# Weight blocks of block one's up-projections written 160 words apart, at another place for each pair, and low activations at another distance in each stage

## The reference

```
def swiglu(x, w_gate, w_up, w_down):
    return (jax.nn.silu(x @ w_gate) * (x @ w_up)) @ w_down

for l in range(DEPTH):                       # block one; DEPTH = 2, D_MODEL = 1024, D_FF = 2816
    h = layer_norm(ALPHA * h + 0.5 * swiglu(h, ffn1_w_gate[l], ffn1_w_up[l], ffn1_w_down[l]), ...)
    proj = h @ w_in[l]                       # state space, two attention mixers
    ...
    h = layer_norm(ALPHA * h + mix, ...)
    h = layer_norm(ALPHA * h + 0.5 * swiglu(h, ffn2_w_gate[l], ffn2_w_up[l], ffn2_w_down[l]), ...)
```

## The kernel before

| operand | start | from block k to k+1 |
|---|---|---|
| `w_hi`, `w_lo` | 128, 0 | 512 bytes, so 0 |
| `x_hi`, `x_lo` (272 or 274 columns) | 192, 64 | 288 words = 1152 bytes, so 128 |
| `plain_hi`, `plain_lo` | 192, 64 | 1152 bytes, so 128 |
| `xt_hi`, `xt_lo` (256 columns) | 64, 64 | 1024 bytes, so 0 |
| `hid_hi`, `hid_lo` (272 columns, down-projections) | 128, 0 | 1088 bytes, so 64 |

## Time and profile before

### The profile page before, as it was taken

One profiled execution on the slowest core, in us unless ns is written; L12 is line 12 of the kernel. 1 busy time (PEld: TensorE's weight loads), 2 busy tenths in 40 slices (PEclk: granted clock), 3 DMA queues, 4 the chain that ended last, 5 costly groups with the idle time before them and its releaser, 6 DMA issues.

```text
span 1951.3 us, 42291 instructions
## 1 busy us (share of the span) xinstructions
PE 1938.8 (99%) x16150; PEld 1899.9 (97%) x16150; DVE 1429.2 (73%) x2591; ACT 1020.5 (52%) x1527; POOL 152.7 (8%) x192
## 2 busy tenths in 40 slices
PE   9999999999999999999999999999999999999998
PEld 9999989999999999899999999999999999999998
DVE  6774787987688758879878875667765775667763
ACT  4443687554455446865546444565445444565443
POOL 0001123000100011320010100000000000100000
PEclk9999999999999999999999999999999999999999
DMA  7454433545454544345553665435564555435554
GB/s 264 172 199 167 165 109 121 182 172 191 154 187 172 186 162 162 109 151 194 187 201 130 230 235 196 152 134 191 193 221 177 194 202 208 151 130 194 194 213 153
DMA packets 46830, 346.66 MB, mean 178 GB/s; under 512 B 5344, under 2 KB 6416, under 8 KB 9232
## 3 DMA queue, kind: packets, MB, share of 16 engines
q1 hardware_dynamic: 44416, 335.63, 47.7%
q0 software_dynamic: 2320, 9.74, 1.5%
HBM read 344.29 MB, written 1.07 MB: 177 GB/s over the span
## 4 chain that ended last, share of the span: by engine, by line
PE 91%; DVE 4%; ACT 2%; DVEq 1%; issue 1%; ACTq 0%; DMA 0%; SPq 0%; POOL 0%
PE ps L595 29%; PE ps L596 29%; PE ps L597 29%; DVE w_lo L1938 1%; PE ps L1111 0%; DVE pj L2399 0%; DVE cst L2420 0%; PE ps L1146 0%; DVE pj L2396 0%; ACT scratch L1615 0%; DVE scratch L2365 0%; PE ps L936 0%; DMA raw<-in_w_up 0%; PE ps L947 0%; ACT w_hi L1246 0%
## 5 line engine op out<-in xcount | busy, mean ns | idle before, releaser
L1938 DVE TENSOR_TENSOR w_lo<-raw,w_hi 128x1024 fp32r<-128x1024 f32 (+1 forms) x582 | 749.6, 1314 | 153.7 <-ACT w_hi L1246 149.7
L1246 ACT ACTIVATE w_hi<-raw 128x1024 fp32r<-128x1024 f32 (+1 forms) x582 | 635.3, 1122 | 118.9 <-PE ps L597 99.3
L595 PE MATMUL ps<-x_hi,w_lo 128*128 128x256 f32 (+3 forms) x2416 | 684.5, 283 | 1.5 <-DVE x_lo L2030 0.6
L596 PE MATMUL ps<-x_lo,w_hi 128*128 128x256 f32 (+3 forms) x2416 | 675.7, 280 | 0.0
L597 PE MATMUL ps<-x_hi,w_hi 128*128 128x256 f32 (+3 forms) x2416 | 675.2, 279 | 0.0
L595 PEld LDWEIGHTS ps<-x_hi,w_lo 128*128 128x128 f32 x2416 | 454.5, 188 | 9.2 <-issue 5.5
L596 PEld LDWEIGHTS ps<-x_lo,w_hi 128*128 128x128 f32 x2416 | 454.0, 188 | 0.8
L597 PEld LDWEIGHTS ps<-x_hi,w_hi 128*128 128x128 f32 x2416 | 454.6, 188 | 0.0
L595 PE MATMUL ps<-hid_hi,w_lo 128*128 128x256 f32 (+1 forms) x1536 | 431.4, 281 | 0.0
L597 PE MATMUL ps<-hid_hi,w_hi 128*128 128x256 f32 (+1 forms) x1536 | 430.2, 280 | 0.0
L596 PE MATMUL ps<-hid_lo,w_hi 128*128 128x256 f32 (+1 forms) x1536 | 429.8, 280 | 0.0
(11 more groups left out here) (330 smaller groups left out, 1554.7 us busy)
## 6 DMA issues: line engine op xcount, KB each, us to landing
raw<-in_w_up SPq DMA_DIRECT2D x176, 1024.0 KB, 4.8
raw<-in_w_down SPq DMA_DIRECT2D x64, 1408.0 KB, 6.0
raw<-in_w_in SPq DMA_DIRECT2D x36, 1024.0 KB, 4.8
raw<-in_w_out SPq DMA_DIRECT2D x16, 1024.0 KB, 4.8
cst<-row_copy POOLq DMA_DIRECT2D x2, 1088.0 KB, 8.5
raw<-in_w_up SPq DMA_DIRECT2D x4, 512.0 KB, 6.7
cst<-in_consts POOLq DMA_DIRECT2D x1, 1537.5 KB, 7.1
prm<-in_prm POOLq DMA_DIRECT2D x2, 690.0 KB, 7.6
```

What stands on the lines that cost most here:

```text
L595: mm(dst, w_lo[:, j, cols], xa, start=first, stop=False)
L596: mm(dst, w_hi[:, j, cols], xb, start=False, stop=False)
L1246: fn(w_hi[:, j, c], raw[:, j, c], ACT.Copy).then_inc(hi_done, 1)
L1938: v.tensor_tensor(w_lo[:, j, c], raw[:, j, c], w_hi[:, j, c].bitcast(F32), ALU.subtract)\
```

## The change

Three things, all in block one's four up-projections.

1. Where the weights' blocks lie. Before, the blocks of a unit stand 128 words apart at the unit's start. Now `placed(turn, j)` gives for the pairs of turns 1 to 10 of each stage (pair n = 0 to 19) a pitch and two offsets, one for `w_hi` and one for `w_lo`. For n below 16 the pitch is 160 words, and the offsets are n modulo 4 and n divided by 4, in units of 64 bytes: each of the 16 combinations once. For n = 16 to 19 the pitch is 128 words, the high offset 0, the low offset 0 to 192 bytes. Turn 0's two pairs and everything outside these stages stay at pitch 128 and offset 0. The second unit of a pair now lies 1408 words (`W_WIDE`) behind the first everywhere. ScalarE and VectorE write the same 1024 words a unit, in these stages as 8 blocks of 128.
2. Where the low activations lie. `plain_lo` starts 2304 words plus 5, 7, 7 or 6 times 64 bytes behind `plain_hi`, by level 0 to 3 (layer 0's ffn2, layer 1's ffn1, layer 1's ffn2, the crossing to block two), where it was 6 times in all four. Modulo 256 bytes the distance is 64, 192, 192 and 128 bytes, where it was 128. The first stage uses `x_hi` and `x_lo`, 128 bytes apart as before.
3. Since a place now depends on the turn, the loops over turns in these four stages are written out on TensorE, ScalarE and VectorE. The loops of the down-projections and of block two stay.

```
+        PLAIN_LO = [KD * X_PITCH + n * LINE for n in (5, 7, 7, 6)]
+        def plain_lo_of(level):
+            return chunks(plain[:, PLAIN_LO[level]:], KD, X_PITCH)
+        STEP = P + 2 * LINE
+        def placed(turn, j):
+            for l in range(DEPTH):
+                for name in ("ffn1", "ffn2"):
+                    t = turn - l * TURNS1 - SEC1[name]
+                    if 1 <= t < UP_T:
+                        n = 2 * t - 2 + j
+                        return (STEP, n % 4 * LINE, n // 4 * LINE) if n < 16 else (P, 0, (n - 16) * LINE)
+            return P, 0, 0
+        def narrow_at(buffer, half, turn, j, u):
+            pitch, *first = placed(turn, j)
+            a = first[half] + u * W_WIDE
+            return chunks(buffer[:, j, a:a + KD * pitch], KD, pitch)[:, :, 0:P]
...
-                    c = u * W_NARROW + k * P
-                    last = three(dst, j, slice(c, c + P), xa[:, k, 0:T], xb[:, k, 0:T], k == 0, k == KD - 1)
+                    if isinstance(turn, int):
+                        high, low = (narrow_at(w, n, turn, j, u)[:, k, :] for n, w in enumerate((w_hi, w_lo)))
+                    else:
+                        c = u * W_WIDE + k * P
+                        high, low = w_hi[:, j, c:c + P], w_lo[:, j, c:c + P]
+                    last = three(dst, high, low, xa[:, k, 0:T], xb[:, k, 0:T], k == 0, k == KD - 1)
...
-                N, xs = T + 2, (plain_hi, plain_lo)
+                N, xs = T + 2, (plain_hi, plain_lo_of(LEVEL_NORM[norm]))
...
-                with pe.Fori(0, (UP_T - 1) // 2) as half:
+                for half in range((UP_T - 1) // 2):
...
+                if isinstance(turn, int) and width == W_NARROW:
+                    fn(narrow_at(w_hi, 0, turn, j, u), narrow_raw(j, u), ACT.Copy).then_inc(hi_done, 1)
...
-                with dve.Fori(0, UP_T - 1) as it:
+                for it in range(UP_T - 1):
```

More of the change, by code:

```diff
@@ L591, in _, with three @@
             tr = nc.tensor.transpose
[L593 to L597, removed]
+            def three(dst, high, low, xa, xb, first, last):
+                mm(dst, low, xa, start=first, stop=False)
+                mm(dst, high, xb, start=False, stop=False)
+                return mm(dst, high, xa, start=False, stop=last)
             def narrow_unit(turn, j, u, dst, T, xs=None, before={}):
@@ L618, in first_pair @@
                     for u in range(2):
-                        c = u * W_NARROW + k * P
-                        last = three(ps[:, bank + u, 0:T], 0, slice(c, c + P), xa[:, k, 0:T], xb[:, k, 0:T],
+                        c = u * W_WIDE + k * P
+                        last = three(ps[:, bank + u, 0:T], w_hi[:, 0, c:c + P], w_lo[:, 0, c:c + P], xa[:, k, 0:T], xb[:, k, 0:T],
                                      n == 0, n == KD - 1)
@@ L660, in up, with four @@
                     narrow_unit(turn0, 1, u, ps[:, 2 + u, 0:T], T, before=before if u == 0 else {})
[L661 removed]
+                def four(half):
                     for i in range(4):
@@ L775, in turn @@
                                 col = u * W_WIDE + c * P
-                                last = three(ps[:, 4 + j, 0:T], j, slice(col, col + P),
+                                last = three(ps[:, 4 + j, 0:T], w_hi[:, j, col:col + P], w_lo[:, j, col:col + P],
                                              ha[:, f, 0:T], hb[:, f, 0:T], f == 0, f == NF - 1)
@@ L1304, in up @@
                     turn(0, W_NARROW)
-                with act.Fori(3 if crossing else 1, UP_T - 1) as it:
-                    turn(it, W_NARROW)
+                if turn0 == SEC1["ffn1"]:
+                    for it in range(1, UP_T - 1):
+                        turn(it, W_NARROW)
+                else:
+                    with act.Fori(3 if crossing else 1, UP_T - 1) as it:
+                        turn(it, W_NARROW)
                 turn(UP_T - 1, W_WIDE)
@@ L1470, in level_up @@
                     pair(0, j, W_NARROW)
-                with act.Fori(1, UP_T - 1) as it:
+                for it in range(1, UP_T - 1):
                     for j in range(2):
@@ L2045, in plain_columns @@
             def plain_columns(level, gain, bias, T):
+                plain_lo = plain_lo_of(level)
                 dve.wait_ge(plain_high_done, level * KD + 1)
```

45 lines of the change are left out of this document (31 added, 14 removed).

## The result

The changed kernel takes 1956.2 us (median of 19 runs, 1955.5 to 1957.7) where the kernel before takes 1953.24 beside it: ratio 1.0015, 95% interval 1.0009 to 1.0020. That is 3.0 us slower, where 4.4 us faster was forecast. The profiled execution took 1955.99 us, its span 1954.2.

A forecast was written before the change was run, and what follows sets the result against it. TensorE's start-to-start time per matmul was taken to bound the kernel. Places gave 4.4 us less, all other parts zero: 1953.2 to 1948.8 profiled, 1949.0 as the median, 8-in-10 range 1940.5 to 1960.5.

The forecast's parts named there:

- One place in four undisturbed, the rest at today's mean: Pitch-160 pairs of block one's up-projections: a quarter of the places run free of the extra, 4.4 us less.
- the floors of 120.0, 120.8 and 114.2: Expected ns per undisturbed matmul with 272, 274 and 258 columns, from block two's 113.3 with 256.
- The prediction's own counter-argument: Down-projection passing four relations and up-projection alternating between two differ by 0.3 ns, which spoke for no net effect of places.
- two columns can't cost 6.7 ns by themselves: Going from 256 to 258 columns should add 0.8 ns of streaming, so the 6.7 seen needed another cause.
- The pairs with pitch 128, and the new distances, at zero: Six pairs a stage with other low offsets or activation distances: the mean over relations stays, so no change.
- The bound of 5.3 us either way: Limit for pitch-128 pairs in the three stages with new distances: 864 matmuls times 6.2 ns, less or more.
- Loops written out, at zero: Block one's up-projections: branches cost TensorE nothing today, so no change; bound 19 us for late fetches.
- Writes as 8 blocks, at zero: Weight writes on VectorE and ScalarE: the same words in runs of 128, spare time hides small extras, no change.
- D: Rival: the writers become the bound, about 1.5 us a pair, 95 us more; chance 0.02 together with late fetches.
- A: Rival: no net effect of places, extra due to columns or activations' step; 1953.4 us, 2 either way; chance 0.28.
- B: Rival: fixed relations make bad places collide in all 8 blocks; 5.9 us more, 1959.3; chance 0.24.
- C: Rival: most places are free, half to all of 17.7 us gained, 1935.7 to 1944.5 us; chance 0.08.

The follow-up runs named there:

- e6_steps: Kernel before with block two's activations stepping 1152 bytes a block and its two ffn2's weights at pitch 160; 1975.17 us in one run.
- e7_columns: Kernel before with block two streaming 258 columns in layer 0's ffn2, 272 in layer 1's ffn1, and weights at pitch 160 in layer 1's ffn2; 1975.14 us.
- e2_places: Changed kernel with low activations back at 128 bytes past the high ones in all stages, places and written-out loops kept; 1954.64 us, ratio 1.0008.
- e1_loops: Changed kernel without weights' places and new distances, so only written-out loops and the second unit's 1408 words remain; 1954.39 us, ratio 1.0002.
- e3_distances: Kernel before with only the low activations at the change's distances, weights and loops untouched; 1952.51 us, ratio 0.9996.
- e8_near: Kernel before with low activations 64 bytes past the high ones in both 274-column stages, 128 elsewhere; 1950.01 us, ratio 0.9984.
- e11_near_place: e8_near with stage 0's weights at pitch 160 and offsets 64 and 64 bytes in every pair; 1949.00 us, ratio 0.9975.
- e9_wide: Kernel before with 288 columns in stages 1 and 2, low activations 64 bytes past in stage 2, and stage 3's chunks 258 words apart; 1966.48 us.
- e5_best_loops: Kernel before, loops and distances kept, with one pitch-160 place a stage: 64 and 64 bytes in three stages, 192 and 192 in the fourth; 1950.66 us.
- e12_written: e8_near with block one's up-projection loops written out and the second unit 1408 words on; 1951.08 us, ratio 0.9989.

## Why the prediction was wrong, point by point

*What bounds the kernel*: right. Every difference in a steady stage is one in TensorE's start-to-start time.

*"One place in four undisturbed, the rest at today's mean"*: this is the step that failed. The inference under it was that block two is fast because weights and activations keep one relation. e6_steps kept the relation and got 117.9 ns; e7_columns changed the weights' steps alone and stayed at 113.5. No pair of any kernel came near the floors of 120.0, 120.8 and 114.2: the best were 123.2, 125.5 and 118.9. Instead of 4.4 us less, the places gave 0.25 more (e2_places over e1_loops), which is no change that the runs can tell. The prediction's own counter-argument (means over two and over four relations differ by 0.3 ns) was the better reading. The other one, that two columns can't cost 6.7 ns by themselves, was simply untrue: in e7_columns they cost 8.

*The pairs with pitch 128, and the new distances, at zero*: too coarse. The distance was one of three edits, and stages 1, 2 and 3 moved by -1.6, +0.2 and +0.7 us at pitch 128 (e3_distances), and by +0.5, +0.5 and +0.4 at pitch 160 (changed over e2_places), 1.4 in all of the 1.56 us between those kernels' medians. The two values of stage 3 are within its own movement of 1.5 us. The bound of 5.3 us either way (864 times 6.2 ns is 5.4) held.

*Loops written out, at zero*: mis-sized. 1.05 and 1.07 us more in two pairs of kernels. The argument looked only at the steady loop, where it was right (stages 1 and 2 of e1_loops are those of before to 0.04 us); the cost lies in the opening (0.4 to 0.75 us, a column that moves by 0.7 by itself) and in layer 1's mixer (0.55 to 0.58 in all four written-out kernels), which the change does not touch, with 0.2 us less in stage 3. e6_steps, with loops, is 0.5 shorter there, so that isn't shown to be a gain of the code.

*Writes as 8 blocks, at zero*: right, 1222 against 1219 ns. D did not happen.

*The sum*: 1.05 for the code, 0.25 for the places at the old distances and 1.56 for the distances on top of them are 2.9 us, of the 3.0 measured. They are steps from one kernel to the next and so add up by construction: they say how the loss divides in this order, and each has the scatter of two medians. In another order the distances alone are worth -0.8 us (e3_distances).

*The rivals*: A was nearest. Good and bad places cancelled; its time of 1953.4, with 2 us either way, lacks the code's cost and that of the distances. The measured 1956.2 is within what the prediction called no change, to which it gave 0.34, against 0.42 for faster. B's price (5.9 us more, pairs near 133 ns) was not reached: the worst pair read 129.9. C was not seen at all. The Trainium skill's rule of independent read ports ("TensorE: Matmul & The Clock Gate", Part 2, Step-by-step) gave A's time. For 256 columns e7_columns agrees with it (113.5 ns with the weights at pitch 128 and at pitch 160). With 272 columns it does not hold: e8_near and e11_near_place differ in stage 0's weights' places alone, and take 124.4 and 123.3 ns there.

## What to carry over

When one stage is slower per instruction than another, change one property of the fast stage on the chip (two columns, one step) before building on an explanation: e6_steps and e7_columns settled here what the profile alone could not. Try a placement as one setting for a whole stage and in repeated runs. Look first at how much the same stage moves between kernels that leave it alone: stage 3 moved by 1.5 us, more than most of the effects looked for. And unrolling is not free because the loop was: look for its price outside the loop, at the next place where engines wait for each other.

## What the runs showed of the hardware

- Matmuls in this three-part pattern take 113.3 to 113.5 ns at 256 columns with activation blocks 1024 bytes apart (before); the same 256 columns with blocks 1152 bytes apart take 118 (e6_steps). With one setting for a whole stage 258 columns take 120.0 to 121.4, 272 take 123.3 to 125.6, 274 take 125.5 to 127.8, 288 take 132 to 134 (e9_wide). So the first two columns above 256 cost 7 to 8 ns and the next 30 some 12, as many as their streaming. What makes the 256-column case special is open.
- The same addresses and code gave 127.8 ns in one stage and 125.6 in another of one execution (e5_best_loops), each steady over 960 matmuls, and 120.0 and 121.0 in the same stage of two kernels (e6_steps, e7_columns). What chooses between the patterns is open too.
- With 274 columns and weights at pitch 128, low activations 64 bytes past the high ones take 125.5 ns where 128 bytes take 127.2. All seven stages so set (e3_distances, e8_near, e12_written, e11_near_place) gave the one, all eight of before, e1_loops, e6_steps and e7_columns the other.
- The executions of e5_best_loops fall into two groups about 2 us apart, 3.4 us from end to end; e11_near_place's lie within 1.1 us.
